# Position embeddings inside the compression products, key slabs ahead of the last queries, HGRN work on other slabs, and two engines that square x

## What is computed

```python
h = rms_norm(x, pre_norm); z = h @ w_in            # split into the names below
# NSA: q of 16 heads; kc vc (compressed), ks vs (selected), kw vw (window), 4 groups of 64
ck = einsum('bcpgd,pde->bcge', kc[:, cidx] + pe_k, w_ck)   # 15 windows of 32 tokens, step 16
cv = einsum('bcpgd,pde->bcge', vc[:, cidx] + pe_v, w_cv)
o_a = (g0*softmax(q ck) cv + g1*softmax(q ks) vs + g2*softmax(q kw) vw) * silu(a)
o_b = pool_mixer(b_v) * silu(b)                    # causal means over 2, 4, 8, 16 tokens
o_c = rms_norm(hgrn2(q, f, i)) * silu(c)           # gated recurrence, 8 heads of 128
out = (sum_n sigmoid(m_n) * (o_n @ w_branch[n])) @ w_out
return x + rms_norm(out, post_norm)
```

## Time and profile before

| | |
|---|---|
| median of 3 runs | 485.43 us (485.16 to 486.59) |
| the profiled execution | 485.57 us, its span 483.8 us |
| mean granted TensorE clock in it | 0.998 of full speed |
| TensorE / VectorE / ScalarE / GpSimd busy | 98 / 71 / 55 / 33% |
| DMA | 76.43 MB, 158 GB/s on average |
| VectorE, positions added to kc and vc (L831) | 16 instructions, 0.41 us each |
| a slab product, 48 matmuls | 5.75 us |

### The profile page before, as it was taken

One profiled execution on the slowest core, in us unless ns is written; L12 is line 12 of the kernel. 1 busy time (PEld: TensorE's weight loads), 2 busy tenths in 40 slices (PEclk: granted clock), 3 DMA queues, 4 the chain that ended last, 5 costly groups with the idle time before them and its releaser, 6 DMA issues.

```text
span 483.8 us, 9621 instructions
## 1 busy us (share of the span) xinstructions
PE 475.2 (98%) x3948; PEld 463.9 (96%) x3948; DVE 343.2 (71%) x577; ACT 264.6 (55%) x398; POOL 159.1 (33%) x157
## 2 busy tenths in 40 slices
PE   9999999999999999899999999999999999999995
PEld 8999999999999999889999999999999999999995
DVE  4898967798976566797896747878584257655653
ACT  6887744594562737553565346576554245433531
POOL 1074820807100009990256415436745120000000
PEclk9999999999999999999999999999999999999999
DMA  8956634454354755555355343253525536677502
GB/s 297 330 170 192 189 103 143 125 171 142 119 175 122 188 137 166 155 164 184 119 187 162 106 133 113 87 156 107 174 89 173 175 120 192 213 233 246 175 1 87
DMA packets 76006, 76.43 MB, mean 158 GB/s; under 512 B 5759, under 2 KB 74751, under 8 KB 75963
## 3 DMA queue, kind: packets, MB, share of 16 engines
q1 hardware_dynamic: 75675, 75.64, 50.4%
q10 hardware_dynamic: 288, 0.18, 0.2%
HBM read 74.77 MB, written 1.05 MB: 157 GB/s over the span
## 4 chain that ended last, share of the span: by engine, by line
PE 94%; DVE 2%; ACT 2%; issue 1%; DVEq 0%; ACTq 0%
PE ps L997 75%; PE ps L1022 4%; PE ps L1160 3%; PE ps L1111 2%; PE ps L1185 1%; PE ps L1100 1%; PE ps L1179 1%; PE ps L1127 1%; DVE WL L629 1%; PE ps L1023 1%; PE ps L1114 1%; PE ps L1038 1%; PE ps L1129 1%; PE ps L1128 1%; PE ps L1065 1%
## 5 line engine op out<-in xcount | busy, mean ns | idle before, releaser
L997 PE MATMUL ps<-hH,WL 128*128 128x256 f32 x688 | 195.6, 288 | 1.2 <-DVE WL L629 1.2
L997 PE MATMUL ps<-hL,WH 128*128 128x256 f32 x688 | 194.8, 284 | 0.0
L997 PE MATMUL ps<-hH,WH 128*128 128x256 f32 x688 | 194.8, 284 | 0.0
L629 DVE TENSOR_TENSOR WL<-W,WH 128x2048 fp32r<-128x2048 f32 (+1 forms) x66 | 152.9, 2317 | 19.5 <-PE ps L997 17.1
L432 ACT ACTIVATE WH<-W 128x2048 fp32r<-128x2048 f32 (+1 forms) x66 | 124.7, 1889 | 47.9 <-PE ps L997 46.6
L997 PEld LDWEIGHTS ps<-hH,WL 128*128 128x128 f32 x688 | 130.6, 191 | 2.3 <-DVE WL L629 1.4
L997 PEld LDWEIGHTS ps<-hL,WH 128*128 128x128 f32 x688 | 131.8, 192 | 0.8 <-issue 0.7
L997 PEld LDWEIGHTS ps<-hH,WH 128*128 128x128 f32 x688 | 131.7, 191 | 0.0
L394 POOL TENSOR_SCALAR R<-R,st 128x256 f32<-128x256 f32 x32 | 29.2, 924 | 82.1 <-DVE st L804 82.1
L997 PE MATMUL ps<-bH,WL 128*128 128x256 f32 x192 | 54.9, 286 | 0.0
L997 PE MATMUL ps<-bH,WH 128*128 128x256 f32 x192 | 54.3, 283 | 0.0
(11 more groups left out here) (192 smaller groups left out, 779.3 us busy)
## 6 DMA issues: line engine op xcount, KB each, us to landing
W<-w_in SPq DMA_DIRECT2D x48, 1024.0 KB, 5.2
W<-w_branch SPq DMA_DIRECT2D x12, 1024.0 KB, 5.3
W<-w_out SPq DMA_DIRECT2D x4, 1024.0 KB, 5.4
W<-w_in SPq DMA_DIRECT2D x2, 608.0 KB, 3.8
R<-x SPq DMA_DIRECT2D x2, 512.0 KB, 4.6
W<-w_in SPq DMA_DIRECT2D x2, 512.0 KB, 6.7
R<-cmp_w SPq DMA_DIRECT2D x2, 512.0 KB, 8.5
OC<-pool_w SPq DMA_DIRECT2D x4, 256.0 KB, 5.9
```

The source lines that it names most:

```text
L629: dve.tensor_tensor(slab_view(WL[:, s % 2], s), slab_view(W[:, s % 3], s), slab_view(WH[:, s % 3], s), ALU.subtract).then_inc(s_lo, 1)
L997: mm = pe.matmul(o, l, r, start=(at == 0 if mixed else k0 + k == 0 and j == 0), stop=(at == len(order) - 1 if mixed else k0 + k == KC - 1 ...
```

## The change

- **Slab order**: vs, q2, kc, vc come before vwk, vw; bv and q are mixed; ks and kw (24, 25) precede q3 (26). In the key slabs VectorE makes the next remainder (`lo(s + 2)`) before it reads the slab.
- **HGRN**: scans at slabs 2, 5, 8, 13; multiplications at 7, 10, 11, 14, 15, 18, 19, 22; roots and normalisations at their own slabs. GpSimd's second chain waits for the first multiplication.
- **Compression**: kc and vc are read by ScalarE without positions, as plain 16-token blocks (`XB`). Positions are a fifth "group": each of the 15 windows has 5 columns, so keys and values have 75 columns (CROWS) in place of 60; the position column of window 0 holds the positions, the others zeros. VectorE fills them in the start. After the products VectorE adds the position column to the keys (CKF); for the values the table SEL adds the position row. CSB is copied at slab 27.
- **Start**: VectorE squares half of x's second row tile, ScalarE the other half; both scale. SP issues the small loads, one between the two halves of x. The first WH and WL are made two chunks at a time.
- **Tail**: the sum over the first three out slabs is made ahead and enters ScalarE's root as its bias.

The diff, cut to its core (the lines that only declare semaphores or repeat a pattern are left out):

```diff
+CROWS = (GROUPS + 1) * NCMP
...
-    out += [("vwk", 0, "in", C_VW), ("vw", 0, "in", C_VW), ("vs", 0, "in", C_VS), ("q", 2, "in", C_Q + 2 * SLAB),
-            ("kc", 0, "in", C_KC), ("vc", 0, "in", C_VC)]
-    out += [("bv", n, "in", C_BV + n * SLAB) for n in range(4)]
-    out += [("q", n, "in", C_Q + n * SLAB) for n in (0, 1, 3)]
-    out += [("ks", 0, "in", C_KS), ("kw", 0, "in", C_KW)]
+    bv, q = ([(kind, n, "in", col + n * SLAB) for n in range(4)] for kind, col in (("bv", C_BV), ("q", C_Q)))
+    out += [("vs", 0, "in", C_VS), q[2], ("kc", 0, "in", C_KC), ("vc", 0, "in", C_VC)]
+    out += [("vwk", 0, "in", C_VW), ("vw", 0, "in", C_VW)]
+    out += bv[0:2] + q[0:2] + bv[2:4] + [("ks", 0, "in", C_KS), ("kw", 0, "in", C_KW), q[3]]
...
-BY_ACT = ("f", "hq", "hv", "vs", "vw", "bv", "q", "ks", "kw", "silu", "merge", "out")
-BY_DVE = ("kc", "vc", "ks", "kw", "q", "silu", "branch", "out")
+BY_ACT = ("f", "hq", "hv", "vs", "vw", "bv", "kc", "vc", "q", "ks", "kw", "silu", "merge", "out")
+BY_DVE = ("ks", "kw", "q", "silu", "branch", "out")
...
-SCAN_AT = (2, 6, 10, 14)
+SCAN_AT = (2, 5, 8, 13)
+MUL_AT = (7, 10, 11, 14, 15, 18, 19, 22)
+RSTD_AT = (15, 19, 22, 26)
+NORM_AT = (16, 20, 23, 27)
...
-        cpe = CP[:, 0:1920].rearrange("p (v j g c) -> p v j g c", v=2, g=GROUPS, c=NCMP)
-        CSB = R[0:GROUPS * NCMP, 2, 1536:1536 + HEAD]
+        XB = CP[:, 0:1280].rearrange("p (v j c g) -> p v j c g", v=2, g=GROUPS + 1, c=T // CS)
+        CSB = R[0:CROWS, 2, 1536:1536 + HEAD]
+        CKF = CP[64:128, 1536:1536 + GROUPS * NCMP].rearrange("p (g c) -> p g c", g=GROUPS)
+        st_cb = st[64:128, 172:173]
...
-        ck_out = ps[64:128, 5, 0:GROUPS * NCMP].rearrange("p (g c) -> p g c", g=GROUPS)
+        ck_all = ps[64:128, 5, 0:CROWS].rearrange("p (c g) -> p g c", c=NCMP)
+        ck_out = ck_all[:, 0:GROUPS]
...
                 sp.dma_start(xin[:, i, :], x[0, P * i:P * i + P, :]).then_inc(s_x[i], 16)
+                if i == 0:
+                    sp.dma_start(K[:, K_ID:K_CMASK], consts[:, K_ID:K_CMASK]).then_inc(s_small, 16)
+            sp.dma_start(V[:], small).then_inc(s_small, 16)
             src = slab_source(0)
...
+                if p == 1:
+                    pool.wait_ge(s_hmul, 1)
...
-                    act.wait_ge(s_cpe, 2)
+                    act.wait_ge(s_ckf, 1)
                     for half in range(2):
-                        last = act.activation(CKS[64 * half:64 * half + 64, 0, :, 0:NCMP], ck_out, ACT.Copy)
+                        last = act.activation(CKS[64 * half:64 * half + 64, 0, :, 0:NCMP], CKF, ACT.Copy)
...
+                elif kind in ("kc", "vc"):
+                    v = 0 if kind == "kc" else 1
+                    for e in range(2):
+                        src = b2[64 * e:64 * e + 64].rearrange("p q (c j k) -> p k q c j", j=CS // 2, k=2)
+                        for k in range(2):
+                            to = XB[64 * k:64 * k + 64, v, :, :, 0:GROUPS].rearrange("p j c (q e) -> p e q c j", e=2)
+                            last = act.activation(to[:, e], src[:, k], ACT.Copy)
+                    last.then_inc(s_read_a, 1)
...
+            act.wait_ge(s_x[0], 16)
+            link(act.activation(sq[:, 0, :], xin[:, 0, :], ACT.Square, accum_out=st_x[:, 0:1]))
+            act.activation(st_t[:, 0:1], st_x[:, 0:1], ACT.Sqrt, scale=1.0 / D, bias=st_eps).then_inc(s_hx, 1)
+            act.wait_ge(s_x[1], 16)
+            link(act.activation(sq[:, 1, D // 2:D], xin[:, 1, D // 2:D], ACT.Square, accum_out=st_x[:, 1:2]))
+            act.wait_ge(s_sq1, 2)
+            act.activation(st_t[:, 1:2], st_x[:, 1:2], ACT.Sqrt, scale=1.0 / D, bias=st_b[:, 0:1]).then_inc(s_hx, 1)
+            act.wait_ge(s_rcp, 1)
+            act.activation(xin[:, 1, 0:D // 2], xin[:, 1, 0:D // 2], ACT.Copy, scale=st_r[:, 1:2]).then_inc(s_xa, 1)
             act.wait_ge(s_first, 16)
-            act.activation(WH[:, 0, 0:FIRST_A, :], W[:, 0, 0:FIRST_A, :], ACT.Copy).then_inc(s_hi0a, 1)
+            act.activation(WH[:, 0, 0:2, :], W[:, 0, 0:2, :], ACT.Copy).then_inc(s_hi0a, 1)
             act.wait_ge(s_small, 32)
             for c in range(KC):
+                if c == 2:
+                    act.activation(WH[:, 0, 2:FIRST_A, :], W[:, 0, 2:FIRST_A, :], ACT.Copy).then_inc(s_hi0a, 1)
...
-                act.wait_ge(s_fin_ss, i + 1)
-                act.activation(st_q[:, i:i + 1], st_t[:, i:i + 1], ACT.Sqrt, scale=1.0 / D,
-                               bias=st_eps).then_inc(s_root, 1)
+                act.wait_ge(s_osq, i + 1)
+                act.wait_ge(s_rest, 1)
+                act.activation(st_q[:, i:i + 1], st_o[:, i, 3:4], ACT.Sqrt, scale=1.0 / D,
+                               bias=st_b[:, i:i + 1]).then_inc(s_root, 1)
...
+                    dve.wait_ge(s_cpe, 2)
+                    dve.tensor_copy(CSB, ps[0:CROWS, 6, 0:HEAD]).then_inc(s_cv, 1)
+                    link(dve.tensor_copy(st_cb, ck_all[:, GROUPS, 0:1]))
+                    dve.tensor_scalar(CKF, ck_out, st_cb, None, ALU.add).then_inc(s_ckf, 1)
+                if s == CK + 1:
                     dve.wait_ge(s_ckh, 1)
                     for half in range(2):
-                        last = dve.tensor_tensor(CKS[64 * half:64 * half + 64, 1, :, 0:NCMP], ck_out,
+                        last = dve.tensor_tensor(CKS[64 * half:64 * half + 64, 1, :, 0:NCMP], CKF,
                                                  CKS[64:128, 0, :, 0:NCMP], ALU.subtract)
                     last.then_inc(s_ck, 1)
-                if s == CV:
-                    dve.wait_ge(s_cpe, 2)
-                    dve.tensor_copy(CSB, ps[0:GROUPS * NCMP, 6, 0:HEAD]).then_inc(s_cv, 1)
...
-                elif kind in ("kc", "vc"):
-                    v = 0 if kind == "kc" else 1
...
+            dve.wait_ge(s_x[1], 16)
+            dve.scalar_tensor_tensor(out=sq[:, 1, 0:D // 2], in0=xin[:, 1, 0:D // 2], scalar=1.0,
+                                     in1=xin[:, 1, 0:D // 2], op0=ALU.mult, op1=ALU.mult,
+                                     accum_out=st_b[:, 1:2]).then_inc(s_sq1, 1)
+            dve.wait_ge(s_sq1, 1)
+            dve.tensor_scalar(st_b[:, 0:1], st_b[:, 1:2], 1.0 / D, EPS, ALU.mult, ALU.add).then_inc(s_sq1, 1)
+            dve.wait_ge(s_hx, 1)
+            link(dve.reciprocal(st_r[:, 0:1], st_t[:, 0:1]))
+            dve.tensor_scalar(xin[:, 0, 0:D // 2], xin[:, 0, 0:D // 2], st_r[:, 0:1], None, ALU.mult).then_inc(s_xn, 1)
+            dve.wait_ge(s_hx, 2)
+            dve.reciprocal(st_r[:, 1:2], st_t[:, 1:2]).then_inc(s_rcp, 1)
+            dve.tensor_scalar(xin[:, 0, D // 2:D], xin[:, 0, D // 2:D], st_r[:, 0:1], None, ALU.mult).then_inc(s_xn, 1)
+            dve.wait_ge(s_rcp, 1)
+            dve.tensor_scalar(xin[:, 1, D // 2:D], xin[:, 1, D // 2:D], st_r[:, 1:2], None, ALU.mult).then_inc(s_xn, 1)
+            for j in range(2):
+                dve.wait_ge(s_hi0a, j + 1)
+                dve.tensor_tensor(WL[:, 0, 2 * j:2 * j + 2, :], W[:, 0, 2 * j:2 * j + 2, :],
+                                  WH[:, 0, 2 * j:2 * j + 2, :], ALU.subtract).then_inc(s_lo0, 1)
...
+            dve.memset(XB[:, :, :, 2:, GROUPS].rearrange("p v j c -> p (v j) c"), 0.0)
+            for v in range(2):
+                for k in range(2):
+                    h = slice(64 * k, 64 * k + 64)
+                    pos = V[h, V_PEK + CB * v:V_PEK + CB * v + CB].rearrange("p (r j k) -> p k j r", r=2, k=2)
+                    last = dve.tensor_copy(XB[h, v, :, 0:2, GROUPS], pos[:, k])
+            last.then_inc(s_pos, 1)
...
-                if mixing(s - 1):
+                if mixing(s - 1) and SLABS[s][0] != "kw":
                     lo(s + 1)
                 mix(s)
+                keys = SLABS[s][0] in ("ks", "kw")
+                if keys:
+                    lo(s + 2)
                 read(s)
                 if s == LAST:
                     merged_lo(3)
-                if s + 2 < NS and not mixing(s):
+                if s + 2 < NS and not mixing(s) and not keys:
...
+            dve.wait_ge(s_read_a, ACT_READS[NS - 2])
+            link(dve.tensor_reduce(st_t, st_o[:, :, 0:3], AX_X, ALU.add))
+            dve.tensor_scalar(st_b, st_t, 1.0 / D, EPS, ALU.mult, ALU.add).then_inc(s_rest, 1)
             for i in range(TT):
                 dve.wait_ge(s_osq, i + 1)
-                dve.tensor_reduce(st_t[:, i:i + 1], st_o[:, i:i + 1, :], AX_X, ALU.add).then_inc(s_fin_ss, 1)
...
-                pe.wait_ge(s_read_v, DVE_READS[WHERE[("vc", 0)]])
+                pe.wait_ge(s_read_a, ACT_READS[WHERE[("vc", 0)]])
+                pe.wait_ge(s_pos, 1)
                 pe.wait_ge(s_hoc, HG)
                 for j in range(CB // 2):
-                    keys, values = (cpe[:, a, j].rearrange("p g c -> p (g c)") for a in range(2))
+                    r = j // (CS // 2)
+                    keys, values = (XB[:, a, j % (CS // 2), r:r + NCMP].rearrange("p c g -> p (c g)") for a in range(2))
                     end = dict(start=(j == 0), stop=(j == CB // 2 - 1))
```

(48 more changed lines are left out.)

26 lines of the change are left out of this document (10 added, 16 removed).

## The result

The changed kernel takes 491.86 us (median of 4 runs, 491.18 to 491.92) against 485.44 for the kernel before beside it: 1.0126 of its time, 95% interval 1.0111 to 1.0141. It is slower by 6.4 us.

A forecast was written before the change was run, and what follows sets the result against it. TensorE, busy 98% of the span, was taken as the bound. Stops -2.4, compression +6.3, start +1.5 and tail -0.15 sum to +5.25 on 485.43: 490.7 us, forecast's own range 488.5 to 492.9, eight in ten 485.3 to 493.0.

The forecast's parts named there:

- Compression: Key and value products on TensorE, 75 columns in place of 60: 8.5 us instead of 2.0, +6.3 us.
- serial passes: In compression, key and value passes run one behind the other instead of side by side: 4.2 us, +2.2.
- turn: In compression, each of 31 changes between 64-wide and full-width weights costs TensorE 0.14 us, 4.3 us together.
- The start: Before the third slab's product: late x, split weight copies and position copies delay it, +1.5 us together.
- The split: In the start, first WH and WL made two chunks at a time: first product ends about 1.0 us later.
- x and the loads: In the start, small loads and VectorE's wait for x's second half make the transposes about 0.25 us later.
- Warm-up matmuls hold TensorE until 8.35 us whatever happens to x: In the start, a fixed bound, so squaring x on two engines has nothing to win.
- The position copies: In the start, VectorE's zeros and four copies of positions precede slab 2's remainder: 1.2 us together.
- HGRN: Slabs 9 to 24: no TensorE stop to win; multiplications nearly late at 14 and 22, 0 to 0.3 us, taken as 0.
- The two stops: Around slab 28: early key slabs with remainders, and CSB's earlier copy, remove TensorE's waits and drains, -2.4 us.
- Rival C: Compression halves still overlap, at most +0.45 us, and the start loses nothing: 483.2 us, chance 0.06.
- Tail: At the end, the last row sum no longer passes through VectorE: -0.15 us.

The follow-up runs named there:

- grouped: Changed kernel with all 16 key products of the compression issued first, then all 16 value products: 488.6 us (1.0073).
- val64: Changed kernel with the compression's value products cut to the first 64 of 75 columns, keys keeping all 75: 487.83 us (1.0081).
- val65: Changed kernel with the compression's value products cut to the first 65 of 75 columns: 491.8 us (1.0125).
- mul: Changed kernel with the odd heads' multiplications at slabs 13 and 21 in place of 14 and 22: 491.08 us (1.0104).
- order_old: Changed kernel with q3 again ahead of the key slabs and their weight remainders behind the key passes: 491.62 us (1.0120).
- swap: Changed kernel with value products turned round: WC's 64 columns as weights, the 75 columns moving; VectorE adds positions and writes replicas: 488.77 us (1.0112).
- best2: Changed kernel with swap, mul, the old start with positions at slab 5, and VectorE work of slabs 26 to 31 lightened: 484.32 us (0.9971).
- best3x: best4 with the old key order: key slabs behind q3, slab 28's remainder behind the key passes: 484.83 us (0.9983).
- best4: best2 with remainders of slabs 29 to 31 ahead of reads, and slab 28's remainder right behind the q3 read: 482.57 us (0.9934).
- start_old: Changed kernel with the earlier start (x squared by ScalarE alone, small loads on its queue, WH/WL in one piece), position copies kept: 489.72 us (1.0087).

## Why the prediction was right, point by point

The forecast was 490.7 us, the result 491.86, inside the forecast's own range (488.5 to 492.9). Between the profiled executions the difference is 6.25 where the sum had 5.25. Against that sum compression is over by 0.39, the start by 0.18, HGRN by 0.73 and the part outside the span by 0.35, the stops are under by 0.49 and the rest by 0.15: the number is as near as it is partly because these cancel.

- **Compression, +6.3; measured +6.69.** The mechanism and both its sizes held: 4.2 for the serial passes (grouped: 4.4, with one turn in it), 0.14 a turn (measured 0.14). val64 and val65 show that it begins with the 65th column, which enters the other half of the array. The Trainium skill (TensorE: Matmul & The Clock Gate, Single matmul latency) gives 166 ns as the warm constant of one matmul's latency, and the prediction's estimate with it at every turn was 491.5. That was nearer the median, but not by its cause: a turn cost 0.14 us, and the rest of the difference lies in the next points.
- **The start, +1.5; measured +1.68 in the span** (1.4 to 1.9 over the seven profiled executions that have this start). The third product began at 23.39, foreseen at 23.3, and as foreseen right behind its remainder; the list of waits, where I had expected an entry for it, has one for the transposes instead. The split (0.6 to 0.9) was priced somewhat high at 1.0; x and the loads (1.2 to 1.3) were not priced well: I had put 0.25 on them, because VectorE would wait for the second half of x. I missed how much earlier than that the first half was ready. "Warm-up matmuls hold TensorE until 8.35 us whatever happens to x" was wrong, see below. The position copies, 1.2 us in my sum, took 0.86 and are free in the shorter start. Three wrong sizes that happened to add up: luck in part.
- **HGRN, booked at 0; measured +0.73.** This is the term that was mis-sized. I had found the two slabs, 14 and 22, worked out "done 8.5 us after the product before, where TensorE wants it at 8.4", and then took the lower end of my own range, 0 to 0.3, of which the upper end would have been short too. The scores were 0.28 late at each, and mul takes back 0.64.
- **The two stops, -2.4; measured -2.89**, of which 0.2 is that the spread's eight matmuls became faster (1.03 to 0.81 us from first to next), with 75 rows of weights instead of 60 and without a stop ahead of them; no run separates the two. The number was right and **the reason half wrong**. I wrote that the key order and the early remainders remove the first stop and that "what is late next there is ScalarE". order_old shows that the stop went even without them, under the longer compression, and grouped, val64 and swap that what is late next is VectorE, with the remainders of slabs 29 to 31. ScalarE has its part in that: in best2 VectorE stood 1.28 us for it. Beside a short compression the reason does hold: best3x against best4.
- **Rival C (483.2 us) left out three things.** It kept the halves side by side and the two stops gone; val64 is nearest to that case and stands at 487.5 to 487.8. Of the 4.3 us between them (487.5) about 2.3 are the start and the HGRN slabs, for which the rival allowed nothing, and 2.1 are val64's two stops for VectorE (1.8 in its waits, 0.16 behind each). As I read it, no row of before shows these because TensorE stood for two other things just ahead of them; that is argued, not shown.
- **Tail, -0.15; measured -0.13**: from the start of the last matmul to that of the last scaling it is 1.61 us before (478.27 to 479.88) and 1.48 after (484.40 to 485.88). No run tests it alone. The other part of the rest's -0.3 is spread over the branch slabs and the last stores and has no cause here; 0.35 us of the difference lies outside the span and has no row.

## What to carry to other kernels

Two small matmuls ran side by side here only while both stayed in their own half of the array; before widening an operand, see on which side it stands, and put the growing one on the moving side. Then ask of every stretch that you shorten what the other engines were doing under it: the 6.5 us that the swap took off TensorE brought 3.1 until a part of VectorE's work went to ScalarE and its remainders were put ahead of reads that wait for a third engine. An edit that measures as nothing may only be hidden by another part of the same change; it is to be tried again once that part is mended.

## What the runs showed of the hardware that I had not expected

- **One column decides.** 64 columns of weights beside a 64-column neighbour: 2.2 us for 64 passes; 65 columns: 8.4; 75 columns: 8.7, and 4.4 when the two widths are not mixed.
- **Behind a stop of TensorE the granted clock can fall.** The windows of val64's profiled execution (microseconds; PE, PEld, DVE, ACT and POOL busy with counts; the granted clock; DMA's share; GB/s):

```profile
220.00:224.00 4.00, 2.45 (x21) 2.25 (x20) 4.00 (x3) 2.54 (x3) 0.80 (x1) 1.00 0.08 26
224.00:228.00 4.00, 4.00 (x24) 4.00 (x23) 3.96 (x5) 1.13 (x2) 0.00 (x0) 0.58 0.79 250
228.00:236.00 8.00, 8.00 (x41) 8.00 (x39) 0.28 (x1) 0.00 (x0) 0.00 (x0) 0.50 0.45 139
236.00:244.00 8.00, 8.00 (x58) 7.91 (x58) 4.43 (x7) 2.70 (x3) 0.00 (x0) 0.86 0.10 32
```

  TensorE stands for 1.55 us until 223.61 and then runs products without a gap. The granted clock is 1.00 until 224, 0.82 from 224 to 225 and 0.50, which is 1.2 GHz, from 225 to 238; it is back at 1.00 from 239. That the stop brings the fall is what the order of the rows suggests; no run here separates it from other causes, and it does not follow every stop: the profiled executions of swap and grouped, which stand 1.13 and 0.87 us before the same slab, have 1.00 behind it.
- **The warm-up's length is not fixed.** Its same 36 passes, first row 1.17, took 7.18 us before, 6.11 after, 5.67 in start_old and 5.91 in best4; mul, whose start is that of the kernel after, took 7.07. The passes start 0.213 us apart at first and 0.111 later, from the 29th on before, the 19th after and the 14th in start_old; the granted clock reads 1.00 in all of these windows, and no run shows what sets the moment. Where they end early, TensorE waits for x (the kernel after: end at 7.28, transposes at 8.74), and an earlier x is worth something; I had read one execution as a bound.
